# Expert stage: the next expert's down weights are split in an expert's last block, and GpSimd's wait for gathered rows moves

## The chip, the cores and the metric

The kernel runs on one core of a Trainium2 chip. Its time is the device time of one execution in microseconds. The core's engines are TensorE (PE; PEld is its weight load), VectorE (DVE), ScalarE (ACT), GpSimd (POOL) and SyncE (SP); each takes its own instructions in order and waits for others through semaphores.

## The reference, cut to what matters

The program is one step of a decoder layer: modulated RMSNorm, an input projection, two mixers, an output projection, and then a mixture of experts. The change lies in the experts alone. For 2056 tokens (2048 of a prompt, 8 samples), a router picks two of 32 experts for each. Each expert computes, on the rows sent to it,

```
def expert_mlp(xb, w1, w3, w2):
    return (jax.nn.silu(xb @ w1) * (xb @ w3)) @ w2
```

with `w1` (gate) and `w3` (up) of 1024 x 512 and `w2` (down) of 512 x 1024, all in fp32. An expert's weights are 6 MB. After the experts, each token's two rows are weighted, added to the residual and normalised.

## The kernel before, in words

Three sets of instructions make up the expert stage, in function `experts`. An expert's rows are cut into blocks of 128, and what is left over after the last full block goes, where it is few enough, into a small block of 32 rows. Experts are walked in order; a "run" is the stretch of experts between two small blocks, so that a small block always stands ahead of the first full block of its expert. How many blocks an expert has, and which have a small one, is known only on the chip: each engine reads it from an SBUF table (`entry`, line 2227, a register load) as it enters a run or an expert.

Precision: an fp32 matrix product is made of three products with shorter operands. ScalarE copies a weight half to `HI` (rounded, line 2344 in `upper(n, e)`), VectorE subtracts it from the raw weights to get `LO` (line 2422 in `lower(n, e)`), and TensorE adds up X_hi\*W_hi, X_lo\*W_hi and X_hi\*W_lo. Index n is 0 for gate, 1 for up, 2 for down; each has two halves of 128 x 2048. The raw weights are tile `WIDE` for gate and up and `W2E` for down; SyncE loads the next expert's half (line 2269) as soon as `LO` of the same half is made, and the small block, which reads raw weights, is done with it. There is one buffer of `HI` and of `LO` for each n.

A full block on TensorE (`block_`): 24 matmuls into `AE` (gate, line 2492), 24 into `BE` (up), six transposes of the next block's gathered rows `XG` into `XP` (line 2481), two transposes of the gated product (`GP`, line 2487), two more of `XP`, two more of `GP`, and 24 matmuls into `YP` (down, line 2497): eight with `HI`, eight with `GL` and `HI`, eight with `LO`. On ScalarE: `SE` = silu(AE) (line 2378), two casts `GH` of `GP` (2382), the cast `XH` of `XP` (2338), two copies `YE` of the output (2388), and its store (2390). On VectorE: `GE` = SE\*BE (2441), `GL` (2445), `XL` (2426). In an expert's last block the next expert's weights are split in between: `HI` of gate behind `SE`, `HI` of up behind `XH`; on VectorE `LO` of gate's first half ahead of `GE`, the rest behind `XL`. The down weights are split at the start of their own expert (`upper(2, e)`, `lower(2, e)`), ahead of `SE` on ScalarE and of everything on VectorE.

A small block (`small`): `AE` and `BE` from raw weights and `XS` (line 2506), `SS` = silu on ScalarE (2360), `GS` on VectorE (2431), a transpose `GP`, its copy `GTS` on ScalarE (2362), then `YP` from raw down weights (2506), `YS` (2368) and four stores (2372).

GpSimd fetches one block ahead (`fetch`): it loads row numbers to `IDX` (2288), waits for them, waits until TensorE has turned the former rows (`gather`), gathers `XG` (2284), and waits until they have landed. Between two runs it does the same for the small block with `IDXS` (2297) and `XGS` (2302). The time ends with a last stage (`combine_and_normalise`), which the change does not touch.

Of the kernel before, what the change touches and what calls it, by code (L numbers as in the profile page):

```python
# [37 lines left out]
KF = DEXP // P  # L38
# [2121 lines left out]
def experts(nc, t, dr, const, state):  # L2160
# [6 lines left out]
    T = SMALL_ROWS  # L2167
    with ExitStack() as ctx:
# [3 lines left out]
        def ps(name, shape):  # L2172
# [25 lines left out]
        sidx_in, sx_in, sx_turned, sx_ready, sa_done, ss_ready, sb_done, sg_ready, sg_turned, sgt_ready, sy_done, sy_taken, sy_out = (  # L2198
            sem(f"small_{x}") for x in ("idx_in", "x_in", "x_turned", "x_ready", "a_done", "s_ready", "b_done", "g_ready", "g_turned", "gt_ready", "y_done",
                                        "y_taken", "y_out"))  # L2200

        first_idx_in, first_x_in, first_turned = sem("first_idx_in"), sem("first_x_in"), sem("first_turned")
        table = state["blocks"]
        SEL, BASE = sb("SEL", [P, ALLT * 2, NEXP]), sb("BASE", [P, ALLT * 2])
        IDXS, IDX0, XG0 = sb("IDXS", [T, 1], I32), sb("IDXS0", [T, 1], I32), sb("XGS0", [T, D])
# [40 lines left out]
        with nc.Block() as block:  # L2246
# [28 lines left out]
            @block.gpsimd  # L2275
            def _(pool):
                def place(value, rows):
                    return nc.s_assert_within(pool.snap(value), 0, NEXP * CAP - rows,
                                              skip_runtime_bounds_check_because="an expert's blocks stay inside its CAP slots")

                def gather(b):
                    pool.wait_ge(x_turned, b + 1)
                    pool.sem_inc(fetching, 1)
                    pool.indirect_dma_start(XG[:], None, dr["h2"], bass.IndirectOffsetOnAxis(ap=IDX[:].bitcast(U32), axis=0)).then_inc(x_in, 16)  # L2284

                def fetch(e, first, skip, b):
                    slot = place(e * CAP + skip + (b - first) * P, P)
                    pool.dma_start(IDX[:], dr["slot"][ds(slot, P), :]).then_inc(idx_in, 16)
                    pool.wait_ge(idx_in, b * 16 + 16)
                    gather(b)  # L2290
                    pool.wait_ge(x_in, b * 16 + 16)

                def fetch_small(e, n):
                    slot = place(e * CAP, T)
                    pool.wait_ge(sx_in, pool.snap(n * 16 - 16))
                    pool.sem_inc(fetching, 1)
                    pool.dma_start(IDXS[:], dr["slot"][ds(slot, T), :]).then_inc(sidx_in, 16)
                    pool.wait_ge(sidx_in, n * 16)

                    pool.wait_ge(sx_turned, n)  # L2300
                    pool.sem_inc(fetching, 1)
                    pool.indirect_dma_start(XGS[:], None, dr["h2"], bass.IndirectOffsetOnAxis(ap=IDXS[:].bitcast(U32), axis=0)).then_inc(sx_in, 16)

                def fetch_expert(e):
                    first, end = bounds(pool, e)
                    skip = entry(pool, 3, e, 0, T)
                    with pool.Fori(first, end) as b:
                        fetch(e, first, skip, b)


                second = place(entry(pool, 0, 1, 1, LAST) * CAP, T)
                pool.dma_start(IDX0[:], dr["slot"][0:T, :]).then_inc(first_idx_in, 16)
                pool.dma_start(IDXS[:], dr["slot"][ds(second, T), :]).then_inc(sidx_in, 16)
                pool.wait_ge(first_idx_in, 16)
                pool.indirect_dma_start(XG0[:], None, dr["h2"], bass.IndirectOffsetOnAxis(ap=IDX0[:].bitcast(U32), axis=0)).then_inc(first_x_in, 16)
                pool.wait_ge(sidx_in, 16)
                pool.indirect_dma_start(XGS[:], None, dr["h2"], bass.IndirectOffsetOnAxis(ap=IDXS[:].bitcast(U32), axis=0)).then_inc(sx_in, 16)
                with pool.Fori(0, runs(pool)) as g:
                    head, behind = run(pool, g)
                    with pool.Fori(head, behind) as e:  # L2320
                        fetch_expert(e)
                    fetch_small(entry(pool, 5, g + 2, 0, LAST), pool.snap(g + 2))
                fetch_expert(LAST)
                blocks = entry(pool, 2, LAST, 1, MAXBLK)
                gather(blocks)

            @block.scalar
            def _(act):
# [45 lines left out]
                def block_(b, n, split):  # L2374
# [7 lines left out]
                        nc.scalar.copy(GH[:, half * 2:half * 2 + 2], GP[half][:]).then_inc(gh_ready, 1)  # L2382
                    take_x(b + 1)
                    split(1)
                    act.wait_ge(y_out, b * 16 + 16)
                    for half in range(2):
                        act.wait_ge(y_done, b * 2 + half + 3)
# [5 lines left out]
                upper(1, 0)  # L2393
                take_small(0)
                small(0, 0, lambda: take_x(0))
                number = runs(act)
                with act.Fori(0, number) as g:
                    head, behind = run(act, g)
                    with act.Fori(head, behind) as e:
                        upper(2, e)  # L2400
                        first, last = first_and_last(act, e)
                        with act.If(last > first):
                            with act.Fori(first, last) as b:
                                block_(b, g + 1, lambda n: None)
                        block_(last, g + 1, lambda n: upper(n, e + 1))
                    small(behind, g + 1)
                upper(2, LAST)
                first, end = bounds(act, LAST)
                with act.Fori(first, end) as b:
                    block_(b, number + 1, lambda n: None)  # L2410
# [6 lines left out]
            def _(dve):  # L2417
# [40 lines left out]
                with dve.Fori(0, number) as g:  # L2458
                    head, behind = run(dve, g)
                    with dve.Fori(head, behind) as e:  # L2460
                        lower(2, e)
                        first, last = first_and_last(dve, e)
                        with dve.If(last > first):
                            with dve.Fori(first, last) as b:
                                block_(b)
                        block_(last, dve.snap(e + 1))
                    small(g + 1)
                lower(2, LAST)
                first, end = bounds(dve, LAST)
                with dve.Fori(first, end) as b:  # L2470
                    block_(b)
                destinations(dve)
# [2 lines left out]
            def _(pe):  # L2475
# [49 lines left out]
                def small(e, n):  # L2525
# [13 lines left out]
                    if static:  # L2539
                        turn_small_g(n)  # L2540
                        turn_small(n + 1)
                        pe.wait_ge(x_in, 16)
                        pe.wait_ge(sx_ready, n + 2)
                        turn_x(range(KD)).then_inc(x_turned, 1)
                    else:
                        pe.wait_ge(xl_ready, first + 1)
                        turn_small(n + 1)
                        pe.wait_ge(gl_ready, first * 2 + 2)
                        turn_small_g(n)
# [12 lines left out]
                def block_(e, b, n):  # L2562
# [10 lines left out]
                    into_hidden(BP[:], XL, HI, 1)  # L2573
                    pe.wait_ge(lo_ready[1], e * 2 + 2)
                    into_hidden(BP[:], XH, LO, 1, last=True).then_inc(b_done, 1)
                    pe.wait_ge(x_in, b * 16 + 32)
                    turn_x(range(6))
                    pe.wait_ge(g_ready, b * 2 + 3)
                    turn_g(0)
# [11 lines left out]
                    into_rows(1, GH, HI, (2, 3))  # L2591
                    pe.wait_ge(gl_ready, b * 2 + 4)
                    for half in range(2):
                        into_rows(half, GL, HI, range(KF))
                    pe.wait_ge(lo_ready[2], e * 2 + 2)
                    for half in range(2):
                        into_rows(half, GH, LO, range(KF), last=True).then_inc(y_done, 1)
# [182 lines left out]
```

## Time and profile before

| | us |
|---|---|
| median of three runs | 2292.2 |
| lowest, highest | 2287.64, 2294.55 |
| the profiled execution's own time | 2288.98 |
| its span in the trace | 2287.5 |
| busy in the span: PE, DVE, ACT, POOL | 1968.3, 1610.8, 1072.1, 565.4 |

Durations are those of the one profiled execution, on a scale that starts with its span. The granted TensorE clock is 0.94 of 2.4 GHz over the whole span. The expert stage begins near 1330 us and its last full block ends near 2177 us. An engine's busy time says little here; what counts is what TensorE waits for, and which chain of waits goes round once in a block.

### The profile page before, as it was taken

The page shows a single profiled execution, that of the slowest core. Times are in us where ns is not written, and L with a number is a line of the kernel's source. Part 1 is how long each engine was busy: PE and PEld are TensorE (multiplying, and loading weights), DVE is VectorE, ACT ScalarE, POOL GpSimd, SP SyncE. Part 2 cuts the span into 40 slices and gives each one's busy share as a digit, 9 for nine tenths or more (in the row PEclk, how much of TensorE's full clock was granted, in tenths as well). Part 3 has the DMA queues.
Part 4 walks back from the last instruction along what each step waited for, and adds up shares of the span by engine and source line. Part 5 has one row for each costly group of instructions (what it writes and reads, how often), then busy time and mean ns, then how long its engine had stood idle before and what let it go on. Part 6 is the DMA issues. An engine that isn't in the chain of part 4 may idle for free. (4 is left out here: it accounts for less than half of the span.)

```text
span 2287.5 us, 40414 instructions
## 1 busy us (share of the span) xinstructions
PE 1968.3 (86%) x13004; PEld 1591.8 (70%) x13005; DVE 1610.8 (70%) x3113; ACT 1072.1 (47%) x2055; POOL 565.4 (25%) x558
## 2 busy tenths in 40 slices
PE   5999999999799998649999849999899999999900
PEld 3788888888577777427888738788777877878700
DVE  2567888889566667749999648766445676658778
ACT  2311111113577778314444237665445665647633
POOL 1024444441011111202655420101110101010066
PEclk7999999999899999869999969999999999999955
DMA  8755555554636448676787549977575978769787
GB/s 260 265 194 201 181 201 202 202 195 155 210 127 225 140 153 283 220 270 199 234 283 247 175 150 369 370 270 300 193 280 190 364 268 303 276 244 388 284 308 290
DMA packets 221577, 553.13 MB, mean 242 GB/s; under 512 B 28973, under 2 KB 43845, under 8 KB 220328
## 3 DMA queue, kind: packets, MB, share of 16 engines
q1 hardware_dynamic: 176272, 434.49, 54.1%
q0 software_dynamic: 24992, 75.13, 8.9%
q10 hardware_dynamic: 20224, 42.38, 5.2%
q8 instruction: 50, 0.82, 0.2%
q14 instruction: 39, 0.32, 0.0%
HBM read 456.86 MB, written 167.63 MB: 273 GB/s over the span
## 5 line engine op out<-in xcount | busy, mean ns | idle before, releaser
L2422 DVE TENSOR_TENSOR LO<-WIDE,HI 128x2048 fp32r<-128x2048 f32 x128 | 287.1, 2285 | 85.3 <-ACT HI L2344 85.3
L599 DVE SCALAR_TENSOR_TENSOR ARENA<-ARENA,TAPW 128x512 f32<-128x512 f32 (+3 forms) x493 | 293.4, 677 | 0.0
L2344 ACT CAST HI<-WIDE 128x2048 fp32r<-128x2048 f32 x128 | 237.8, 1909 | 18.7 <-PEq L199 16.2
L425 POOL TENSOR_TENSOR MS<-SSQ,K 128x1 f32<-128x1 f32 x17 | 167.8, 9869 | 295.2 <-ACT H L468 295.2
L2422 DVE TENSOR_TENSOR LO<-W2E,HI 128x2048 fp32r<-128x2048 f32 x64 | 143.8, 2289 | 93.5 <-ACT HI L2344 93.5
L718 PE MATMUL PJ<-WIN_H,HTH 128*128 128x512 f32 x680 | 173.4, 398 | 15.3 <-ACT HTH L474 11.7
L1044 ACT ACTIVATE PR<-SBX,NM 128x256 f32<-128x256 f32 (+1 forms) x384 | 171.9, 456 | 2.6 <-DVE NM L976 2.6
L722 PE MATMUL PJ<-WIN_H,HTL 128*128 128x512 f32 x680 | 169.7, 392 | 0.0
L726 PE MATMUL PJ<-WIN_L,HTH 128*128 128x512 f32 x680 | 168.1, 390 | 0.0
L500 ACT ACTIVATE ARENA<-PJ 128x512 f32<-128x512 f32 x51 | 30.4, 598 | 288.7 <-PE PJ L726 288.7
L718 PEld LDWEIGHTS PJ<-WIN_H,HTH 128*128 128x128 f32 x680 | 127.9, 190 | 46.5 <-ACT HTH L474 15.9
L722 PEld LDWEIGHTS PJ<-WIN_H,HTL 128*128 128x128 f32 x680 | 129.2, 190 | 27.2
L2344 ACT CAST HI<-W2E 128x2048 fp32r<-128x2048 f32 x64 | 119.2, 1910 | 61.1 <-issue 61.1
L726 PEld LDWEIGHTS PJ<-WIN_L,HTH 128*128 128x128 f32 x680 | 127.7, 188 | 26.5
L2284 POOL DMA_INDIRECT XG<-h_rows,IDX x41 | 47.2, 1150 | 330.2 <-PE XP L2481 263.3
L973 DVE CUSTOM_DVE_ANT_0 SBX<-S,WAD 128x256 f32<-128x256 f32 (+1 forms) x256 | 88.0, 400 | 33.9 <-issue 31.4
L1163 PE MATMUL OT<-PTS,VN 128*64 128x128 f32 x1200 | 90.2, 282 | 20.7 <-DVE PTS L986 20.7
L1140 PE MATMUL TB<-K,PR 128*128 128x128 f32 x600 | 85.4, 278 | 8.3 <-ACT PTS L1031 8.3
L1163 PEld LDWEIGHTS OT<-PTS,VN 128*64 128x64 f32 x1200 | 63.3, 136 | 41.5 <-issue 22.3
L942 POOL DMA_DIRECT2D branch_rows<-O x44 | 23.7, 540 | 266.6 <-ACT O L1025 266.6
L2492 PE MATMUL AE<-HI,XH 128*128 128x512 f32 x320 | 81.7, 398 | 8.6 <-issue 8.6
L2382 ACT CAST GH<-GP 128x256 fp32r<-128x256 f32 x80 | 29.8, 372 | 126.3 <-PE GP L2487 123.8
(341 smaller groups left out, 4359.5 us busy)
## 6 DMA issues: line engine op xcount, KB each, us to landing
WIDE<-in_w_expert_gate SPq DMA_DIRECT2D x64, 1024.0 KB, 7.5
WIDE<-in_w_expert_up SPq DMA_DIRECT2D x64, 1024.0 KB, 9.9
W2E<-in_w_expert_down SPq DMA_DIRECT2D x64, 1024.0 KB, 9.2
expert_rows<-YE ACTq DMA_DIRECT2D x40, 512.0 KB, 6.2
expert_rows<-NOROWS POOLq DMA_DIRECT2D x11, 1536.0 KB, 11.7
X<-in_x_prompt SPq DMA_DIRECT2D x31, 512.0 KB
WAD<-in_w_ada SPq DMA_DIRECT2D x13, 1024.0 KB, 8.6
QN<-q_rows SPq DMA_DIRECT2D x48, 256.0 KB, 3.0
```

The lines of the kernel that those rows point to most:

```text
L425: pool.tensor_tensor(MS[:], SSQ[:], const("eps"), ALU.add).then_inc(ms_ready, 1)
L599: ins = nc.vector.scalar_tensor_tensor(out=out, in0=src, scalar=tap, in1=out, op0=ALU.mult, op1=ALU.add)
L718: nc.tensor.matmul(PJ[:, n], HTH[:, k], WH[:, n, k], start=k == 0, stop=False)
L722: nc.tensor.matmul(PJ[:, n], HTL[:, k], WH[:, n, k], start=False, stop=False)
L726: mm = nc.tensor.matmul(PJ[:, n], HTH[:, k], WL[:, n, k], start=False, stop=k == KD - 1)
L973: nc.vector.tensor_tensor_reduce(SBX[hh][:, h, 0:wide], SP_[hh][:, at_bank(h), 0:wide], bias, 1.0, -3e38, ALU.add, ALU.max, ml[:, head:hea ...
L1044: ins = nc.scalar.activation(PR[hh][:, h, 0:w], SBX[hh][:, h, 0:w], ACT.Exp, bias=NM[:, head:head + 1], scale=1.0, accum_out=ML[g.q][:, HE ...
L1140: mm = nc.tensor.transpose(TB[u % 2][:, n], PR[head // HH][:, head % HH, k * P:(k + 1) * P], const("ident"))
L1163: mm = nc.tensor.matmul(OT[s * DH:(s + 1) * DH, pair], VN[(q - nk + 1 + k) % 4][:, head * DH:(head + 1) * DH], PTS[:, u, n], start=k == 0, ...
L2344: nc.scalar.copy(HI[n][:, cols], raw[n][:, cols]).then_inc(hi_ready[n], 1)
L2422: nc.vector.tensor_tensor(LO[n][:, cols], raw[n][:, cols], HI[n][:, cols], ALU.subtract).then_inc(lo_ready[n], 1)
L2492: mm = nc.tensor.matmul(out, x[:, k], w[n][:, k * DEXP:(k + 1) * DEXP], start=first and k == 0, stop=last and k == KD - 1)
```

## The change

On ScalarE, `upper(2, e + 1)` runs in the last block of expert e, behind `upper(1, e + 1)` and ahead of the two `YE` copies; it waits on a new semaphore, `down_used`, which TensorE raises after its last matmul of a block that reads `HI` of down. `upper(2, 0)` runs after the first small block, and the calls at an expert's start are gone. On VectorE, `lower(2, e)` stands where it was, at the start of its expert, but behind the table loads, and it waits for `y_done` of the block before. On GpSimd, the wait for the landed `XG` stands ahead of the next load of `IDX` instead of right behind the gather; the first load of row numbers counts on the same semaphore, which shifts its counts by 16.

```diff
                 def fetch(e, first, skip, b):
                     slot = place(e * CAP + skip + (b - first) * P, P)
+
+                    pool.wait_ge(x_in, b * 16 + 16)
+                    pool.sem_inc(fetching, 1)
                     pool.dma_start(IDX[:], dr["slot"][ds(slot, P), :]).then_inc(idx_in, 16)
                     pool.wait_ge(idx_in, b * 16 + 16)
                     gather(b)
-                    pool.wait_ge(x_in, b * 16 + 16)
...
                     take_x(b + 1)
                     split(1)
+                    split(2)
                     act.wait_ge(y_out, b * 16 + 16)
...
                 small(0, 0, lambda: take_x(0))
+                upper(2, 0)
                 number = runs(act)
+
+                def split_next(n, e, b):
+
+                    if n == 2:
+                        act.wait_ge(down_used, b + 1)
+                    upper(n, e + 1)
+
                 with act.Fori(0, number) as g:
                     head, behind = run(act, g)
                     with act.Fori(head, behind) as e:
-                        upper(2, e)
                         first, last = first_and_last(act, e)
...
-                        block_(last, g + 1, lambda n: upper(n, e + 1))
+                        block_(last, g + 1, lambda n: split_next(n, e, last))
                     small(behind, g + 1)
-                upper(2, LAST)
...
                     with dve.Fori(head, behind) as e:
+                        first, last = first_and_last(dve, e)
+
+                        dve.wait_ge(y_done, first * 2 + 2)
                         lower(2, e)
-                        first, last = first_and_last(dve, e)
...
                     for half in range(2):
-                        into_rows(half, GL, HI, range(KF))
+                        mm = into_rows(half, GL, HI, range(KF))
+                    mm.then_inc(down_used, 1)
                     pe.wait_ge(lo_ready[2], e * 2 + 2)
```

In ScalarE's program, the end of an expert's last block, before: `XH`, the next up weights' casts, the output copies and their store, then the loop's end.

```order
L2338 CAST XH<-XP 128x1024
L2344 CAST HI<-WIDE 128x2048 x2
L2385 ISA
L2388 COPY YE<-YP 128x512 x2
L2390 ISA
L2390 DMA expert_rows<-YE 128x1024
L2399 REGISTER_ALU
L2399 COMPARE_AND_BRANCH
```

The same place now:

```order
L2343 CAST XH<-XP 128x1024
L2349 CAST HI<-WIDE 128x2048 x2
L2349 CAST HI<-W2E 128x2048 x2
L2391 ISA
L2394 COPY YE<-YP 128x512 x2
L2396 ISA
L2396 DMA expert_rows<-YE 128x1024
L2413 REGISTER_ALU
L2413 COMPARE_AND_BRANCH
```

The two down casts have come in ahead of the copies and the store. In the same program, the start of an expert (the loop over the experts of a run), before; the table loads are `TENSOR_LOAD blocks`.

```order
L2399 ISA
L2344 CAST HI<-W2E 128x2048 x2
L2227 ISA
L2227 TENSOR_LOAD blocks
L2227 ISA x3
L2227 TENSOR_LOAD blocks
L2227 ISA x2
L2402 REGISTER_ALU
L2402 COMPARE_AND_BRANCH
```

And now:

```order
L2413 ISA
L2228 TENSOR_LOAD blocks
L2228 ISA x3
L2228 TENSOR_LOAD blocks
L2228 ISA x2
L2415 REGISTER_ALU
L2415 COMPARE_AND_BRANCH
```

The two table loads used to stand behind the casts; now nothing is ahead of them but the store of the former block.

## Rows read from the trace of the kernel before

**Rows 1.** Experts' stretch: length; busy PE, PEld, DVE, ACT, POOL; clock; DMA share; GB/s.

```profile
1355.00:2170.00 815.00, 783.82 (x4886) 638.05 (x4887) 530.92 (x393) 488.58 (x461) 86.13 (x97) 0.99 0.79 292
```

**Rows 2.** PE's waits there: us in total, times, longest.

```profile
PE XP L2481 <- DMA XG<-h_rows,IDX: 15.3, 3, 6.8
PE GP L2487 <- DVE GE L2441: 5.4, 6, 1.1
PE YP L2506 <- ACT GTS L2362: 4.0, 9, 0.4
```

**Rows 3.** Timeline of a block ahead of a single-block expert: start, us, engine, operation.

```profile
1387.64 0.60 ACT L2378 ACTIVATE SE<-AE 128x512 f32<-128x512 f32 x1
1388.13 3.70 ACT L2344 CAST HI<-WIDE 128x2048 fp32r<-128x2048 f32 x2
1390.27 2.29 DVE L2422 TENSOR_TENSOR LO<-WIDE,HI 128x2048 fp32r<-128x2048 f32 x1
1393.15 0.75 DVE L2441 TENSOR_TENSOR GE<-SE,BE 128x256 f32<-128x256 f32 x2 [0.60 <-PE BE L2492]
...
1395.72 3.72 ACT L2344 CAST HI<-WIDE 128x2048 fp32r<-128x2048 f32 x2
...
1400.38 0.59 ACT L2388 COPY YE<-YP 128x512 f32<-128x512 f32 x1 [0.26 <-PE YP L2497]
1401.24 0.38 ACTq L2390 DMA_DIRECT2D expert_rows<-YE  x1
1402.08 3.73 ACT L2344 CAST HI<-W2E 128x2048 fp32r<-128x2048 f32 x2 [1.11 <-issue]
...
1405.82 0.60 ACT L2378 ACTIVATE SE<-AE 128x512 f32<-128x512 f32 x1
```

**Rows 4.** TensorE's two late transposes of gathered rows.

```profile
1651.32 1.54 PE L2481 MATMUL XP<-K,XG 128*128 128x128 f32 x6 [5.50 <-DMA XG<-h_rows,IDX]
...
1926.76 0.87 PE L2481 MATMUL XP<-K,XG 128*128 128x128 f32 x6 [2.96 <-DMA XG<-h_rows,IDX]
```

**Rows 5.** GpSimd's gathers: two behind the small block at 1627, one of 1920.

```profile
1632.19 0.86 POOL L2302 DMA_INDIRECT XGS<-h_rows,IDXS  x1 [17.94 <-PE XP L2518]
...
1642.73 2.88 POOL L2284 DMA_INDIRECT XG<-h_rows,IDX  x1 [5.83 <-DMA IDX<-slot_tokens]
...
1920.28 1.04 POOL L2284 DMA_INDIRECT XG<-h_rows,IDX  x1 [5.47 <-DMA IDX<-slot_tokens]
```

**Rows 6.** Timeline around the small block at 1627.

```profile
1622.53 3.72 ACT L2344 CAST HI<-WIDE 128x2048 fp32r<-128x2048 f32 x2
...
1628.01 0.34 ACTq L2390 DMA_DIRECT2D expert_rows<-YE  x1
...
1629.25 0.28 ACT L2360 ACTIVATE SS<-AE 128x128 f32<-128x128 f32 x1 [1.50 <-PE AE L2506]
1630.89 0.29 DVE L2431 TENSOR_TENSOR GS<-SS,BE 128x128 f32<-128x128 f32 x1 [0.38 <-PE BE L2506]
1632.07 1.93 PE L2506 MATMUL YP<-W2E,GTS 128*32 128x256 f32 x32 [0.45 <-ACT GTS L2362]
...
1638.33 3.72 ACT L2344 CAST HI<-W2E 128x2048 fp32r<-128x2048 f32 x2 [3.84 <-issue]
1640.27 4.49 DVE L2422 TENSOR_TENSOR LO<-W2E,HI 128x2048 fp32r<-128x2048 f32 x2 [9.09 <-ACT HI L2344]
```

**Rows 7.** ScalarE's table loads in 1636.6 to 1638.3, before the casts: min/median/max ns.

```profile
L2227 ACTq TENSOR_LOAD <-blocks x2: 280/280/281, 1637.0 to 1637.6; - x2
```

**Rows 8.** The gathers of `XG` in 1355 to 2170, ns, and their landing.

```profile
L2284 POOL DMA_INDIRECT XG<-h_rows,IDX x40: 944/972/3047, 1362.8 to 2146.1; - x40
...
DMA to landing us min/median/max: 4.0/6.7/8.8
```

**Rows 9.** SyncE's loads of down weights: one pair, and the landing of all.

```profile
1388.29 2.46 SPq L2269 DMA_DIRECT2D W2E<-in_w_expert_down  x2
...
DMA to landing us min/median/max: 4.8/9.2/10.9
```

More of the change, by code:

```diff
@@ L2200, in experts @@
                                         "y_taken", "y_out"))
-        first_idx_in, first_x_in, first_turned = sem("first_idx_in"), sem("first_x_in"), sem("first_turned")
+        down_used = sem("down_hi_used")
+        first_x_in, first_turned = sem("first_x_in"), sem("first_turned")
         table = state["blocks"]
@@ L2311, in _ @@
                 second = place(entry(pool, 0, 1, 1, LAST) * CAP, T)
-                pool.dma_start(IDX0[:], dr["slot"][0:T, :]).then_inc(first_idx_in, 16)
+                pool.dma_start(IDX0[:], dr["slot"][0:T, :]).then_inc(x_in, 16)
                 pool.dma_start(IDXS[:], dr["slot"][ds(second, T), :]).then_inc(sidx_in, 16)
-                pool.wait_ge(first_idx_in, 16)
+                pool.wait_ge(x_in, 16)
                 pool.indirect_dma_start(XG0[:], None, dr["h2"], bass.IndirectOffsetOnAxis(ap=IDX0[:].bitcast(U32), axis=0)).then_inc(first_x_in, 16)
@@ L2324, in _ @@
                 blocks = entry(pool, 2, LAST, 1, MAXBLK)
+                pool.wait_ge(x_in, blocks * 16 + 16)
                 gather(blocks)
@@ L2467, in _ @@
                     small(g + 1)
+                first, end = bounds(dve, LAST)
+                dve.wait_ge(y_done, first * 2 + 2)
                 lower(2, LAST)
-                first, end = bounds(dve, LAST)
                 with dve.Fori(first, end) as b:
@@ L2541, in small @@
                         turn_small(n + 1)
-                        pe.wait_ge(x_in, 16)
+                        pe.wait_ge(x_in, 32)
                         pe.wait_ge(sx_ready, n + 2)
@@ L2575, in block_ @@
                     into_hidden(BP[:], XH, LO, 1, last=True).then_inc(b_done, 1)
-                    pe.wait_ge(x_in, b * 16 + 32)
+                    pe.wait_ge(x_in, b * 16 + 48)
                     turn_x(range(6))
```

## The prediction

> **What bounds the kernel now.** I read the busy time by stretch first, then TensorE's waits, then the timeline of single blocks. In the 815 us of the experts TensorE is busy for 783.8 us at a granted clock of 0.99, with 0.79 of the DMA engines' time taken [rows 1]. So TensorE sets the pace, and what the change can give is what TensorE now waits: 15.3 us for gathered rows in three waits, of which the first, 6.8 us, is the start of the stage; 5.4 us for `GE` in six; 4.0 us for `GTS` in nine [rows 2]. No wait for `HI`, `LO` or raw weights of the down projection is among them. The nine waits for `GTS` are the nine small blocks behind the first, so small blocks are places where TensorE has nothing to do while ScalarE works.
>
> The timeline gives a second picture, the loop that ScalarE and VectorE go round once in a block. From one `SE` to the next it is 1405.82 - 1387.64 = 18.18 us [rows 3], which is TensorE's own period of a block. `GE` is made ready by TensorE: VectorE sat idle 0.60 us for `BE` ahead of it [rows 3]. That 0.60 us is all the slack that this loop has in a single-block expert, since there VectorE makes `LO` of the next gate's first half between `SE` and `GE`.
>
> **The row numbers on GpSimd.** The two late transposes inside the stage (5.50 and 2.96 us) [rows 4] hang on this chain: TensorE turns the small block's rows, the gather of `XGS` starts (1632.19, waited 17.94 us for TensorE), table loads, the load of `IDX`, its landing, the gather of `XG` at 1642.73 [rows 5]. The wait that the change moves stands before the 17.94 us of waiting and is hidden by it. The row numbers of a small block will be loaded some 5 to 7 us earlier and nothing behind it starts earlier. Elsewhere the gathers already wait for TensorE. Gain: 0; an added semaphore step in each fetch lies in the same waits.
>
> **The down split: small blocks.** Ahead of a small block, ScalarE's casts of `HI` for up start at 1622.53 and last 3.72 us [rows 6]. Now two more casts of the same length follow (2 x 3.72 = 7.44, to 1629.97), then two copies `YE` of 0.59 us. Neighbours overlap by about 0.1 us (`SE` starts at 1387.64, lasts 0.60, and its successor starts at 1388.13 [rows 3]), so the copies end near 1630.9. The store starts 0.27 us behind the last copy (1400.38 + 0.59 to 1401.24 [rows 3]), near 1631.15, and `SS` 1.24 us behind the store (1628.01 to 1629.25 [rows 6]), near 1632.4 in place of 1629.25. It lasts 0.28 us, and `GS` follows near 1632.7 in place of 1630.89: 1.8 us late. From `GS` to TensorE's `YP` nothing has room (1.18 us, and TensorE sat idle for `GTS` [rows 6]), so TensorE loses 1.8 us. Bounds: 1.6 if the 1.24 us holds some waiting for `AE`, 2.2 if nothing overlaps. Nine small blocks: **+16.2** (14.4 to 19.8). The next down weights must have landed for this; see the rivals.
>
> **The down split: what goes.** Behind a small block, `HI` and `LO` of down are now ready or in work before the block begins; before, the casts stood at 1638.33, ahead of `SE` [rows 6]. That is what made `GE` late in six blocks, by up to 1.1 us [rows 2]; all six waits are in the first block behind a small one. The casts kept `SE` back until 1642.05 (1638.33 + 3.72); without them it can start about 2 us earlier, even with its table loads bare. Gain: **-5.4** (at least -4).
>
> **Gathered rows after that.** In both places of [rows 4] a small block stands between the fetch and the late transpose, so 1.8 us of each wait is filled by the small block's new delay, which costs nothing there: 5.50 becomes 3.7, 2.96 becomes 1.2. Besides, the gather at 1642.73 took 2.88 us, three times the median of 0.972, and lay beside `LO` of down, which stood there from 1640.27 for 4.49 us [rows 6] and will now follow `GS` and be done by 1638; landing in the median 6.7 us in place of the 8.5 that its late start and the transpose at 1651.32 give takes off 1.8 more [rows 4, 5, 8]. At 1920 the gather was near its normal length and only its transfer has less company: I take 0.6 off. Sum: 8.46 less (1.9 + 0.6) = **-6.1**; bounds -3.6 (only the filling) and -8.5 (all of it goes).
>
> The Trainium skill speaks against the middle part of this. "SBUF — State Buffer", under "Practical consequences", says that a `tensor_tensor` with two SBUF inputs takes only the read side of the interface shared with GpSimd, and infers that making descriptors needs the write side, so that this operation did not stall a DMA. By that rule the 2.88 us is not `LO`'s doing and the sum would be 1.8 us higher. This trace speaks for a hold-up: the longest gathers [rows 8] all lie beside a `LO`.
>
> **The down split: single-block experts.** This is the part that is easy to miss. The two table loads of an expert ran under the down casts; now they stand bare between the store and `SE`. From `HI` of up at 1395.72: 7.44 us of casts, 1.18 of copies, less 0.3 of overlap, to 1404.1; the store at 1404.4; then 0.84 us as now from the store to what follows it (1401.24 to 1402.08 [rows 3]); then two loads of 0.28 us each, with their register steps 1.33 us (1637.0 to 1638.33 [rows 6, 7]); and 0.25 us for the branch and the row address. `SE` at 1406.8 in place of 1405.82: 1.0 us late. From `SE` to the earliest `GE` is 0.49 + 2.14 + 2.29, less 0.1 of overlap, 4.8 us [rows 3], so `GE` at 1411.6 to 1411.7 where TensorE has it due at 1393.15 + 18.18 = 1411.33. The loop becomes 18.5 us long and TensorE waits 0.3 to 0.4 us in each round. An expert pays it if it has one full block and no small block: 15 such experts by the order of `SE` and down casts in the trace, the first with casts at 1383.91, the last at 2134.88. At 0.35: **+5.2**. Bounds: 0, if a few tenths of my steps overlap, and 0.8 each, 12, if the loads or the branch take twice as long. An expert of several blocks does not pay, since its first block has no `LO` ahead of `GE`.
>
> The output copies come 3.5 us later, but TensorE needs `YP` only in the next block's last third, so that is free. VectorE's `LO` of down ends 8 us into the block as before.
>
> **Sum.** 16.2 - 5.4 - 6.1 + 5.2 = +9.9 us on the profiled execution's 2288.98, which is 2298.9. That execution lies 3.2 us below the median of the runs, so the forecast for a median is 2292.2 + 9.9 = **2302**.
>
> **Rivals.**
> - The loop of single-block experts keeps pace (0 in place of 5.2). For it: 0.3 us is less than the sum of what I read off in six steps. Against: all six steps are in the rows. +4.7: 2297. Chance 0.20.
> - The down weights land late. A pair is issued at 1388.29, the second half near 1390.4 [rows 9]; the casts now want them near 1399.4 and 1401.2. With the median landing of 9.2 us there are 1.6 us left; with the longest, 10.9, the cast waits 0.1 us, and a queue with less room would make it more. In single-block experts each tenth goes into the loop. At 0.7 us more in 15: +20, 2312. Chance 0.14.
> - The other side: the late `SS` is not what TensorE waits for in a small block, and the five or more us of `GE` and the row waits go in full. TensorE's waits would fall by 8.5 + 5.4 = 13.9, and at 0.5 us for each small block the sum is -9.4: 2283. It decides from the point where a small block costs less than 1.5 us. Against it: in [rows 6] only 1.2 us lie between `GS` and `YP`, and all of it is work. Chance 0.06.
> - The gather at 1642.73 stays long for a reason other than `LO`: 1.8 us of the row waits stay, +11.7, 2304. Chance 0.10. The Trainium skill's rule named above ("SBUF — State Buffer") would have it so.
>
> **How the numbers follow.** My case has 0.50, with a range of its own of 2297 to 2308. The low sum of all bounds is 14.4 - 5.4 - 8.5 + 0 = +0.5, the high one 19.8 - 4 - 3.6 + 12 = +24.2: 2293 to 2316. The range reaches from 2293 to 2315; the case of the other side is left out. A measurement of this kernel can tell about 0.3%, 6.9 us, from no change: below 2285.3 is faster, above 2299.1 slower. Slower: most of my case and of the long gather's, and the late weights, 0.67. The same: the loop that keeps pace and the low end of my case, 0.27. Faster: 0.06.
>
> **What would show it.** In the new profile `GTS` waits of TensorE should be about 2.2 us each, nine times, in place of 0.45. The waits for `GE` behind small blocks should be gone, and some 15 of 0.3 us should stand in their place, with `SE` 6.8 us into a block in place of 5.9. The wait of GpSimd for TensorE ahead of `XGS` should be longer and the transposes near 1651 and 1927 late by 2 us and 1 us. I am wrong on the mechanism if the nine `GTS` waits stay near 0.45 us, or if TensorE now waits for `HI` or `LO` of down.

## The result and the profile after

The changed kernel takes 2297.15 us, the median of 13 runs (2292.87 to 2302.28); the kernel before takes 2290.7 us in 13 runs of the same sittings (2282.33 to 2294.55). The ratio is 1.0038, with a 95% interval of 1.0028 to 1.0048: the change costs 8.7 us (6.4 to 11.0), where +9.9 was forecast. The profiled execution of the new kernel spans 2295.4 us, that of before 2287.5.

TensorE's waits in the experts' stretch (1355 to 2190) show the exchange. Columns: what waited and for what, us in total, times, longest.

```profile
PE GP L2538 <- DVE GS L2443: 14.7, 9, 1.7
PE XP L2496 <- DMA XG<-h_rows,IDX: 9.8, 3, 5.9
PE AE L2507 <- issue: 5.0, 6, 1.5
PE YP L2521 <- ACT GTS L2367: 4.0, 9, 0.4
PE GP L2502 <- DVE GE L2453: 0.9, 3, 0.4
```

Against [rows 2], the wait for gathered rows is down from 15.3 to 9.8 us (0.9 of this at the start of the stage, 6.8 against 5.9), that for `GE` from 5.4 to 0.9. A new line stands on top: in each of the nine small blocks TensorE now waits up to 1.7 us for `GS`. The wait for `GTS` is what it was. There is no wait for `HI` or `LO` of down. The wait "for issue" of 1.5 us is that ahead of the stage's first full block; the others, 0.7 to 0.8 us each, stand ahead of a full block behind a small one.

A small block, start, us, engine and operation, to be laid beside [rows 6]:

```profile
1621.84 3.72 ACT L2349 CAST HI<-WIDE 128x2048 fp32r<-128x2048 f32 x2
1625.45 3.72 ACT L2349 CAST HI<-W2E 128x2048 fp32r<-128x2048 f32 x2
...
1626.40 1.95 PE L2521 MATMUL AE<-WIDE,XS 128*32 128x128 f32 x64
...
1630.39 0.34 ACTq L2396 DMA_DIRECT2D expert_rows<-YE  x1
...
1631.63 0.28 ACT L2365 ACTIVATE SS<-AE 128x128 f32<-128x128 f32 x1 [1.50 <-issue]
1631.94 0.29 DVE L2443 TENSOR_TENSOR GS<-SS,BE 128x128 f32<-128x128 f32 x1 [2.12 <-ACT SS L2365]
1632.38 0.30 PE L2538 MATMUL GP<-K,GS 128*128 128x128 f32 x1 [1.66 <-DVE GS L2443]
1633.12 3.45 PE L2521 MATMUL YP<-W2E,GTS 128*32 128x256 f32 x32 [0.45 <-ACT GTS L2367]
...
1635.89 4.49 DVE L2434 TENSOR_TENSOR LO<-W2E,HI 128x2048 fp32r<-128x2048 f32 x2 [3.66 <-issue]
1636.50 2.22 PE L2507 MATMUL AE<-HI,XH 128*128 128x512 f32 x8
```

`SS` follows `HI` of up by 9.79 us; the forecast's steps give 1632.4 - 1622.53 = 9.87. TensorE stands 1.66 us for `GS`. Then something that no step of the forecast had: the 32 matmuls of `YP` take 3.45 us, where those of before took 1.93 [rows 6].

The windows of the same trace say why. Columns: stretch, length, busy PE, PEld, DVE, ACT, POOL, granted clock, DMA share, GB/s. The first lies behind the small block above, the second behind another one of the same kernel.

```profile
1634.00:1637.00 3.00, 3.00 (x27) 1.52 (x19) 1.11 (x1) 0.33 (x1) 0.58 (x1) 0.53 0.98 363
1750.00:1753.00 3.00, 3.00 (x13) 2.50 (x14) 2.91 (x2) 0.00 (x0) 0.00 (x0) 1.00 1.04 413
```

A clock of 0.53 is nearly all at the lower level, 1.2 GHz. Such a stretch of 3.4 us stands behind four of the nine small blocks (at 1633.4, 1848.4, 1913.3 and 1944.0), where the 32 matmuls take 3.00 to 3.45 us; the other five run them in 1.93 us, as all nine did before. Where the stretch begins late, it reaches into the next full block, whose first eight matmuls then take up to 2.65 us in place of 2.09:

```profile
1850.68 2.62 PE L2507 MATMUL AE<-HI,XH 128*128 128x512 f32 x8
```

A block ahead of a single-block expert, to be laid beside [rows 3]:

```profile
1398.44 1.98 PE L2507 MATMUL AE<-HI,XH 128*128 128x512 f32 x8
...
1402.56 0.38 ACTq L2396 DMA_DIRECT2D expert_rows<-YE  x1
...
1405.02 0.60 ACT L2383 ACTIVATE SE<-AE 128x512 f32<-128x512 f32 x1 [2.74 <-PE AE L2507]
...
1407.45 2.29 DVE L2434 TENSOR_TENSOR LO<-WIDE,HI 128x2048 fp32r<-128x2048 f32 x1 [1.10 <-ACT HI L2349]
1409.66 0.74 DVE L2453 TENSOR_TENSOR GE<-SE,BE 128x256 f32<-128x256 f32 x2
...
1416.64 1.98 PE L2507 MATMUL AE<-HI,XH 128*128 128x512 f32 x8
```

`SE` follows the store by 2.46 us with no cast between: those are the bare table loads. `GE` follows `SE` by 4.64 us and VectorE no longer sits idle for `BE` ahead of it, so the slack of 0.60 us [rows 3] is used up. Yet TensorE's round is 1416.64 - 1398.44 = 18.20 us, hardly longer than the 18.18 of before. It becomes clearly longer only where the loads themselves are slow, as in the block that starts at 2084.02, a round of 18.62 us:

```profile
2091.02 0.60 ACT L2383 ACTIVATE SE<-AE 128x512 f32<-128x512 f32 x1 [3.17 <-issue]
...
2096.12 0.44 PE L2502 MATMUL GP<-K,GE 128*128 128x128 f32 x2 [0.40 <-DVE GE L2453]
```

The two table loads there, and all of the stretch (min/median/max ns):

```profile
L2228 ACTq TENSOR_LOAD <-blocks x2: 452/579/706, 2089.0 to 2089.8; - x2
```
```profile
L2228 ACTq TENSOR_LOAD <-blocks x87: 273/285/761, 1385.3 to 2169.6; - x87
```

Of the 15 rounds of single-block experts, two are 0.44 and 0.47 us longer than before (mean of their two loads 0.53 and 0.58 us) and four are 0.16 to 0.21 us longer (0.42 to 0.48 us). The other nine, with loads of 0.38 us or less in the mean, are longer by at most 0.07 us.

Of [rows 4], the two late transposes are still late, by 2.29 and 1.59 us in place of 5.50 and 2.96, and the gathers of [rows 8] are all short now:

```profile
1650.07 1.23 PE L2496 MATMUL XP<-K,XG 128*128 128x128 f32 x6 [2.29 <-DMA XG<-h_rows,IDX]
...
1929.25 0.87 PE L2496 MATMUL XP<-K,XG 128*128 128x128 f32 x6 [1.59 <-DMA XG<-h_rows,IDX]
```
```profile
L2285 POOL DMA_INDIRECT XG<-h_rows,IDX x40: 946/972/982, 1361.5 to 2152.6; - x40
```

To size each term I took the starts of TensorE's blocks in each trace (the first matmul of every `AE`, and of `YP` in small blocks) and summed the distances by kind, from the first full block's start to the last one's. The same blocks are in the same column for every kernel; all in us.

| kernel | small: `AE` to `YP` (9) | small: `YP` to next `AE` (9) | first block | six blocks that waited for `GE` | two blocks that waited for rows | 15 single-block experts | rest | total |
|---|---|---|---|---|---|---|---|---|
| before | 45.17 | 23.52 | 19.77 | 115.57 | 46.99 | 272.77 | 272.92 | 796.71 |
| after | 60.19 | 25.85 | 18.28 | 110.91 | 42.37 | 274.69 | 272.80 | 805.09 |
| difference | +15.0 | +2.3 | -1.5 | -4.7 | -4.6 | +1.9 | -0.1 | +8.4 |

The 8.4 us covers what the two spans differ by (7.9) and agrees with the ratio (8.7), so the change acts in this stretch.

The first block's 1.5 us is no wait. Its first eight matmuls ran at the lower clock in the trace of before and not in the new one:

```profile
1362.23 3.54 PE L2492 MATMUL AE<-HI,XH 128*128 128x512 f32 x8 [2.44 <-issue]
```
```profile
1361.98 2.10 PE L2507 MATMUL AE<-HI,XH 128*128 128x512 f32 x8 [1.45 <-issue]
```

The granted clock in 1362 to 1365 is 0.50 before and 1.00 after.

### The profile page after: what moved, and what is told of

It is laid out like the page before. It is cut to its first block and busy times, and to the rows that moved or that the text cites. A ratio compares the mean times of both kernels' runs of the same rounds, so it can differ in the third digit from the quotient of the medians.

```text
span 2295.4 us, 40488 instructions
## 1 busy us (share of the span) xinstructions
PE 1976.1 (86%) x13004; PEld 1595.9 (70%) x13005; DVE 1610.3 (70%) x3113; ACT 1063.1 (46%) x2055; POOL 556.4 (24%) x558
## 5 line engine op out<-in xcount | busy, mean ns | idle before, releaser
L2349 ACT CAST HI<-WIDE 128x2048 fp32r<-128x2048 f32 x128 | 237.3, 1909 | 16.2 <-PEq L199 16.2
L2285 POOL DMA_INDIRECT XG<-h_rows,IDX x41 | 39.8, 971 | 451.5 <-PE XP L2496 424.3
L2383 ACT ACTIVATE SE<-AE 128x512 f32<-128x512 f32 x40 | 24.0, 599 | 152.9 <-PE AE L2507 123.9
L2512 PE MATMUL YP<-HI,GH 128*128 128x512 f32 x320 | 83.7, 404 | 4.6
```

The costliest lines, as they stand in the source:

```text
L2349: nc.scalar.copy(HI[n][:, cols], raw[n][:, cols]).then_inc(hi_ready[n], 1)
L2512: mm = nc.tensor.matmul(YP[:, half * 512:half * 512 + 512], g[:, k], w[2][:, k * D + half * 512:k * D + half * 512 + 512], start=first and ...
```

## The experiments

Theory A, from the prediction: the casts ahead of small blocks cost, their absence behind small blocks gains, the loop of single-block experts is at its limit, and GpSimd's edit is worth nothing. Rivals: the cost is GpSimd's and not the split's; the loop has slack left and the loss is all in small blocks; the long gathers are not `LO`'s doing; the half clock behind small blocks is what the runs' difference is made of. The first four kernels stand beside the same runs of before (median 2290.64 us), and so do the last four (2287.32 us).

| kernel | median us | ratio to before, 95% interval | profiled span |
|---|---|---|---|
| pool_only | 2287.11 | 0.9984 [0.9968, 0.9999] | 2288.6 |
| split_only | 2300.32 | 1.0041 [1.0022, 1.0061] | 2305.4 |
| casts_in_small | 2284.79 | 0.9974 [0.9959, 0.9989] | 2288.3 |
| loads_doubled | 2321.42 | 1.0133 [1.0107, 1.0160] | 2320.6 |
| inner_early | 2282.74 | 0.9978 [0.9961, 0.9994] | 2284.6 |
| warm | 2295.44 | 1.0027 [1.0009, 1.0045] | 2298.3 |
| numbers_early | 2278.97 | 0.9964 [0.9948, 0.9980] | 2275.2 |
| all_moves | 2269.96 | 0.9926 [0.9899, 0.9953] | 2263.6 |

And their blocks, in the columns of the table above. It is one trace each, so a column moves by chance too; and the column of single-block experts holds one late transpose of the first run in split_only (about 2.0 us) and in casts_in_small (9.1 us), which is no loss of the loop.

| kernel | small `AE` to `YP` | `YP` to `AE` | first | six `GE` | two rows | 15 single | rest | total |
|---|---|---|---|---|---|---|---|---|
| pool_only | 45.15 | 23.65 | 19.85 | 115.13 | 49.29 | 272.89 | 272.92 | 798.88 |
| split_only | 60.68 | 27.52 | 19.78 | 111.96 | 40.48 | 279.16 | 272.84 | 812.42 |
| casts_in_small | 45.17 | 23.50 | 18.27 | 111.32 | 47.37 | 281.86 | 272.84 | 800.33 |
| loads_doubled | 59.90 | 26.55 | 18.29 | 110.17 | 43.46 | 299.83 | 272.84 | 831.04 |
| inner_early | 45.16 | 23.64 | 19.91 | 110.11 | 48.96 | 275.93 | 272.76 | 796.47 |
| warm | 60.83 | 23.68 | 19.64 | 109.78 | 45.56 | 276.44 | 272.81 | 808.74 |
| numbers_early | 45.18 | 23.50 | 19.88 | 115.41 | 38.65 | 272.66 | 272.84 | 788.12 |
| all_moves | 45.18 | 23.55 | 18.31 | 111.41 | 37.82 | 272.63 | 272.81 | 781.71 |

### The two parts apart: pool_only and split_only

pool_only is the kernel before with GpSimd's edit alone:

```diff
 def fetch(e, first, skip, b):
     slot = place(e * CAP + skip + (b - first) * P, P)
+    pool.wait_ge(x_in, b * 16 + 16)
+    pool.sem_inc(fetching, 1)
     pool.dma_start(IDX[:], ...).then_inc(idx_in, 16)
     pool.wait_ge(idx_in, b * 16 + 16)
     gather(b)
-    pool.wait_ge(x_in, b * 16 + 16)
```

> The kernel before with GpSimd's edit alone. My theory: the moved wait stands ahead of a wait for TensorE (17.94 us at 1632), so TensorE's time does not change: 0, and the transposes near 1651 and 1927 are late by 5.5 and 3.0 us as before. Rival (the edit removes row waits): both waits go, -8.5 us.

Measured: 0.9984 [0.9968, 0.9999]. Its trace shows the waits of before in sum, three for rows of 15.4 us together and six for `GE`:

```profile
PE XP L2484 <- DMA XG<-h_rows,IDX: 15.4, 3, 6.6
...
PE GP L2490 <- DVE GE L2444: 4.8, 6, 0.8
```

So the cost of the change isn't in this edit. The two late transposes wait 8.8 us together, for 8.5 before, as forecast; but one by one they are not those of before:

```profile
1648.05 1.54 PE L2484 MATMUL XP<-K,XG 128*128 128x128 f32 x6 [3.11 <-DMA XG<-h_rows,IDX]
...
1925.32 1.54 PE L2484 MATMUL XP<-K,XG 128*128 128x128 f32 x6 [5.66 <-DMA XG<-h_rows,IDX]
```

The long gather has changed places with them: 1.02 us at 1641.60 and 3.08 us at 1916.36, for 2.88 and 1.04 in [rows 5]. Whether the edit gains up to 0.3% in another way is at the limit of what the runs tell.

split_only is the new kernel with the same lines put back as they were before; the down split stays.

> The changed kernel with GpSimd's part undone. My theory: as slow as the changed kernel, +8 to +9 us against before, with nine waits of 1.6 us for GS in small blocks. Rival (GpSimd's part gave something back): 3 us or more slower than the changed kernel.

Measured: 1.0041 [1.0022, 1.0061], +9.4 us, which is all of the change's cost. The rival, a kernel 3 us slower than the changed one, lies inside the interval and isn't excluded. In its trace `AE` to `YP` of the small blocks is 60.68 us, as in the new kernel, so that +15 belongs to the split. Its waits:

```profile
PE GP L2535 <- DVE GS L2440: 15.0, 9, 1.7
PE XP L2493 <- DMA XG<-h_rows,IDX: 12.7, 5, 6.9
```

Two things are different from the new kernel. There are five waits for rows in place of three; one of the new ones (1.91 us, at 1470.66) stands in the first run of experts. And the half clock stands behind eight of the nine small blocks (`YP` to next `AE` 27.52 us).

### Where the down casts of a small block's expert should stand: casts_in_small

The kernel before, with one group of casts moved: those for an expert that comes behind a small block are made inside it, behind `SS`, where ScalarE has room. All others stay at the start of their expert.

```diff
@@ small, on ScalarE
         meanwhile()
+    upper(2, e)
     act.wait_ge(sy_out, n * 64 + 64)
@@ loop over experts
-    upper(2, e)
+    with act.If(e > head):
+        upper(2, e)
@@ ahead of the last expert
-upper(2, LAST)
```

> The kernel before, but the down casts of an expert with a small block run in that small block, behind ScalarE's copies of GTS, XS and XH; all other experts cast at their start as before. My theory (the changed kernel's gain is the six GE waits and the held-up gather, its cost the late SS): no GS waits, no GE waits, the gather near 1643 back at 1.0 us and its wait down from 5.5 to about 3.7: -5.4 - 1.9 - about 1 at the first block = -7 to -8 us. Rival (the GE waits come from something else than the order on ScalarE): 0.

Measured: 0.9974 [0.9959, 0.9989], -6.0 us for the -7 to -8 expected. This takes the split's gain without its price: `AE` to `YP` stays at 45.17 us, the six blocks fall to 111.32, and TensorE waits 0.8 us for `GE`:

```profile
PE XP L2482 <- DMA XG<-h_rows,IDX: 20.9, 4, 6.7
...
PE GP L2488 <- DVE GE L2442: 0.8, 4, 0.2
```

The trace itself is no shorter than before's in this stretch (800.33 against 796.71), because of a wait for rows in the first run that the trace of before doesn't have:

```profile
1468.36 1.54 PE L2482 MATMUL XP<-K,XG 128*128 128x128 f32 x6 [6.74 <-DMA XG<-h_rows,IDX]
```

GpSimd ahead of it:

```profile
1443.64 0.56 POOL L2297 DMA_DIRECT2D IDXS<-slot_tokens  x1 [9.06 <-issue]
1449.14 1.28 POOL L2302 DMA_INDIRECT XGS<-h_rows,IDXS  x1 [4.93 <-DMA IDXS<-slot_tokens]
1453.26 0.58 POOL L2288 DMA_DIRECT2D IDX<-slot_tokens  x1 [2.84 <-issue]
1459.72 2.31 POOL L2284 DMA_INDIRECT XG<-h_rows,IDX  x1 [5.89 <-DMA IDX<-slot_tokens]
```

Four steps stand in a row, and a gather of 2.31 us beside `LO` ends them. In the new kernel, with GpSimd's edit, the first of these is 12 us earlier and the gather waits for TensorE:

```profile
1431.34 0.56 POOL L2300 DMA_DIRECT2D IDXS<-slot_tokens  x1 [0.54 <-issue]
...
1448.07 0.97 POOL L2285 DMA_INDIRECT XG<-h_rows,IDX  x1 [5.59 <-PE XP L2496]
```

That is where GpSimd's edit has a use: it gives the first run's fetches 12 us of room that they need only sometimes. Both kernels whose trace has this wait lack the edit; that the edit's small gain in pool_only is made of it is likely, but wasn't shown.

### Does the loop of single-block experts have slack: loads_doubled

The new kernel, with the two table loads ahead of `SE` made twice:

```diff
     with act.Fori(head, behind) as e:
+        first_and_last(act, e)
         first, last = first_and_last(act, e)
```

> The changed kernel with the two table loads at an expert's start done twice on ScalarE, 1.3 us more between store and SE. If the loop SE, HI, LO, GE, HI, HI, SE has used up its slack, as its GE now stands 0.07 us behind TensorE's pace, each of 15 single-block experts without a small block pays 1.2 to 1.3 us: +18 us on the changed kernel, and more waits of TensorE for GE. Rival (TensorE sets the pace there with room to spare): 0 to +3 us.

Measured: 1.0133 [1.0107, 1.0160], 24 us above the new kernel in medians, for the +18 expected. The 15 single-block experts take 299.83 us, 25.1 more than in the new kernel, 1.68 each, and nothing else moved by more than 1.1. TensorE's waits for `GE`:

```profile
PE GP L2503 <- DVE GE L2454: 21.4, 15, 2.3
```

Fifteen waits for `GE`, as many as there are such experts: more time on ScalarE between the store and `SE` goes into TensorE's time, so the loop has no slack left in the new kernel. The forecast had the mechanism and the count right and the size too low. The waits are 1.43 us each; the rest of the loss is mostly the clock, which was at 0.50 to 0.53 in 3 us behind three of the longest of them (2.26, 1.60 and 2.14 us), where the round took 1.4 to 1.7 us more than its wait. The new kernel's own loss there is small because it stands just at the limit.

### The new kernel without its casts ahead of small blocks: inner_early

Here the new kernel keeps the early split between two experts of a run, and makes that for a small block's expert inside the small block. The call `upper(2, 0)` behind the first small block is gone too (not shown below).

```diff
@@ small, on ScalarE
+    upper(2, e)
@@ split_next
-    if n == 2:
-        act.wait_ge(down_used, b + 1)
-    upper(n, e + 1)
+    if n < 2:
+        upper(n, e + 1)
+    else:
+        with act.If(behind > act.snap(e + 1)):
+            act.wait_ge(down_used, b + 1)
+            upper(2, act.snap(e + 1))
```

> The changed kernel, but an expert with a small block has its down casts in that small block, behind ScalarE's copies; only experts without one keep the split in the block before. My theory: the small blocks' 15 us and the half-clock stretches behind them are gone, and what is left against the kernel with casts in small blocks alone is the loop of single-block experts, 0.05 to 0.4 us in each of 15, +1 to +5 us on it, about -3 to 0 us against before. Rival (the whole loss came from the small blocks): the same time as casts in small blocks alone, -6 us.

Measured: 0.9978 [0.9961, 0.9994], -5.0 us for the -3 to 0 expected, against 1.0038 for the new kernel: the casts ahead of small blocks, with what follows from them, cost 0.6%. `AE` to `YP` is back at 45.16 and `YP` to `AE` at 23.64 us, so the half clock has gone with the wait. The 15 experts take 275.93, 3.2 more than before: in this trace, the loop's price alone. Its waits:

```profile
PE XP L2499 <- DMA XG<-h_rows,IDX: 15.3, 3, 6.9
PE GP L2505 <- DVE GE L2456: 2.2, 3, 1.0
```

The waits for rows are back at 15.3 us, 8.4 of it in the two late transposes (6.9 is the first), although the down `LO` is made early here too and the gather is short. The first of the two, GpSimd's step and TensorE's:

```profile
1639.63 0.97 POOL L2285 DMA_INDIRECT XG<-h_rows,IDX  x1 [5.61 <-DMA IDX<-slot_tokens]
```
```profile
1647.07 1.54 PE L2499 MATMUL XP<-K,XG 128*128 128x128 f32 x6 [4.27 <-DMA XG<-h_rows,IDX]
```

The other waits 4.18 us, for 2.96 before, although its gather was short both times. So one wait of one trace tells little, and the two late transposes have to be read over several kernels. Where the gather was long (2.88 and 3.08 us: before, pool_only) they waited 5.50 and 5.66 us. Where it was short and the small blocks as before (before, pool_only, casts_in_small, inner_early) the six waits lie between 2.96 and 4.27 us, 3.7 in the mean. Where it was short and the small block late (the new kernel, split_only, loads_doubled, warm) the eight lie between 1.49 and 3.77 us, 2.2 in the mean. So the long gather costs some 1.8 us, and the small block's delay fills some 1.5 us of each wait, which is no true gain. In time inner_early and casts_in_small can't be told apart.

### Is it the clock: warm

The new kernel, with five matmuls of 512 columns that nobody reads, in the small block's wait for `GS`. They add work and take none out.

```diff
     turn_small(n + 1)
+    pe.wait_ge(hi_ready[0], e * 2 + 2)
+    pe.wait_ge(y_taken, first * 2 + 2)
+    pe.wait_ge(sy_taken, n + 1)
+    for k in range(5):
+        nc.tensor.matmul(YP[:, 0:512], XH[:, k], HI[0][:, ...], start=k == 0, stop=k == 4)
```

> The changed kernel with five matmuls of 512 columns, whose result is thrown away, in the wait for GS of each small block. The wait of 1.65 us is still there as time. If the half clock behind small blocks (four stretches of 3.4 us in the changed kernel's trace) comes from TensorE's idling there, no such stretch is left and the time falls by 3 to 5 us on the changed kernel. Rival (the clock falls for another reason, or the filler delays more than it saves): stretches remain, 0 to +3 us on the changed kernel.

Measured: 1.0027 [1.0009, 1.0045]. In the trace the half clock is gone from behind all nine small blocks, and `YP` to next `AE` takes 23.68 us in place of 25.85:

```profile
1631.23 1.43 PE L2567 MATMUL YP<-HI,XH 128*128 128x512 f32 x5
...
1633.74 1.93 PE L2521 MATMUL YP<-W2E,GTS 128*32 128x256 f32 x32 [0.45 <-ACT GTS L2367]
```
```profile
1634.00:1637.00 3.00, 2.33 (x35) 1.47 (x28) 0.28 (x1) 0.37 (x1) 0.00 (x0) 1.00 0.94 315
```

So it is the idle time in the small block that lets the clock fall. Its price in the new kernel's trace is 2.3 us between `YP` and `AE` and some 1.1 us in two of the six blocks behind (18.83 and 18.87 us in place of 18.3; none over 18.33 in warm). `AE` to `YP` is unchanged at 60.83: most of the cost is the late `GS` and not the clock. By the ratios warm is 2.5 us faster than the new kernel, for the 3 to 5 expected, but the two intervals overlap, so the runs don't show it; and its trace as a whole is 3.7 us longer, by waits for rows (6.2 us for 3.9), the first block and the loop.

### What the late gathers really wait for: numbers_early

The kernel before; the row numbers of the next run's first block are loaded ahead of GpSimd's wait for the turned small rows, not behind it. This is the wait of 17.94 us in [rows 5] that the change's own edit doesn't pass.

```diff
 def fetch_small(e, n, following):
     ...
     pool.dma_start(IDXS[:], ...).then_inc(sidx_in, 16)
+    first_numbers(following)
     pool.wait_ge(sidx_in, n * 16)
     pool.wait_ge(sx_turned, n)
@@ fetch
+    with pool.If(b > begun):
+        numbers(e, first, skip, b)
     pool.wait_ge(idx_in, b * 16 + 16)
     gather(b)
```

> The kernel before, but GpSimd loads the row numbers of the next run's first block ahead of its wait for the small block's rows to be turned. My theory: the late transposes near 1651 and 1927 hang on the chain turned, gather, table loads, row numbers, gather; with the row numbers there beforehand both waits (5.5 and 3.0 us) go, and the odd one in the first run: -8 to -10 us. Rival (the gathers' transfers are what is late): less than -3 us.

Measured: 0.9964 [0.9948, 0.9980], -8.2 us, at the near end of the -8 to -10 expected. The two blocks with late rows fall from 46.99 to 38.65 us. That this 8.3 is nearly the 8.46 of [rows 4] is chance: the waits are gone, and with them some 1.6 us of lower clock behind the longer one (the clock was 0.56 in 1652 to 1656 before), but two waits for `GE` of 0.81 and 0.90 us, which they had covered, came out. Beyond the start of the stage there is no wait for rows left:

```profile
PE GP L2498 <- DVE GE L2452: 6.9, 8, 1.0
```

The chain of [rows 5] is thus shown to be the cause of those waits.

### Together: all_moves

The kernel before with the three edits that gained or did no harm: casts_in_small, the change's own edit on GpSimd, and numbers_early.

> Casts in small blocks, GpSimd's deferred wait, and the early row numbers together, on the kernel before. The waits for GE and for rows are different stretches, so the gains add up: -6 (casts) - 7 (rows, less what the casts already gave there) = -12 to -15 us. Rival (what one gives, the next wait takes): no better than the better of the two alone.

Measured: 0.9926 [0.9899, 0.9953], 2269.96 us: 17 us faster than before, for the -12 to -15 expected, and the fastest of all. The single ratios add up to 0.9974 + 0.9964 + 0.9984 - 2 = 0.9922. TensorE's waits for `GE`:

```profile
PE GP L2501 <- DVE GE L2455: 2.0, 7, 0.5
```

The row numbers stand ready before the gather, and a gather beside `LO` (1.92 us) no longer matters, since it starts 5.25 us behind the start of `XGS` in place of 10.54 [rows 5]:

```profile
1621.29 0.90 POOL L2312 DMA_INDIRECT XGS<-h_rows,IDXS  x1 [20.50 <-issue]
1626.54 1.92 POOL L2284 DMA_INDIRECT XG<-h_rows,IDX  x1 [4.35 <-issue]
```

## Why the prediction was right, and where it was not

The forecast of +9.9 us and the measured +8.7 (6.4 to 11.0) agree, and the median of 2297.15 us lies in the stated range, 4.9 us under the 2302 named (1.5 of it because the median of before fell to 2290.7 with more runs). The largest term and its mechanism are the ones foretold. That the sum comes out so near is in part luck: of the new kernel's trace, the single-block experts are 3.3 us less than forecast, and the clock, which was in no term, is about as much more. The chance of 0.67 was for more than 2299.1 us, which the median doesn't reach; that the kernel is slower is clear only because 13 runs of each give a narrow interval. Point by point:

- **Small blocks, +16.2.** Measured +15.0, 1.67 each for 1.8. Shown by split_only (there) and by inner_early (gone with the casts). The sign foretold was the wrong one: the new wait shows at the transpose of `GS`, with 14.7 us in nine, while the nine waits for `GTS` stay at 0.45, which the prediction had named as proof that its mechanism was wrong. `GTS` is made from what TensorE transposes, so it can't take on a delay that comes from `GS`; the mechanism held, and the sign didn't follow from it.
- **`GE` behind small blocks, -5.4.** Measured -4.7, which holds about +1.1 of the lower clock; without that stretch the same six blocks gain 5.8 (warm) and 5.5 (inner_early). casts_in_small gets 4.3 alone, without the early split.
- **Gathered rows, -6.1.** Measured -4.6, within its bounds (its own terms, 8.46 less 1.9 and 0.6, give -6.0 and not -6.1). Both parts are there: the gather did get shorter (2.88 us became 0.97), worth some 1.8 us by the waits of all traces, as foretold, and the small block's delay laid over the waits took some 1.5 us from each, for 1.8. The waits of one trace scatter by as much as these parts, so the nearness of the sum says less than they do.
- **Single-block experts, +5.2.** This is the term that was mis-sized: measured +1.9 in the new kernel, nearer to the rival's 0 than to the forecast, 3.2 and 3.7 in inner_early and warm. `SE` was as late as foretold (0.94 us for 1.0; it stands 6.58 us into the block for 5.64, where the prediction has 6.8 for 5.9). But `GE` follows it by 4.64 us, not 4.8, which leaves a normal round 0.02 us long; only rounds with slow table loads pay more, two of them 0.4 to 0.5 and four about 0.2, and three waits for `GE` show in place of 15. The step that failed was the difference of two nearly equal times, each with some 0.1 us of reading error. loads_doubled shows the mechanism itself, and that the loop, where it keeps pace, does so only by a hair.
- **The clock.** No term of the sum had it. It costs 2.3 us between `YP` and the next `AE` in the new kernel's trace (4.0 in split_only) and about 1.1 in the blocks behind, and warm shows its cause.
- **The first block, -1.5.** In the trace of before its first matmuls ran at the lower clock. It is near 19.8 us in six of the ten traces, with 3.18 to 3.63 us for these eight matmuls, and near 18.3 in the other four, with 2.09 to 2.11. warm, which has all of the change, is among the six, so it is chance and not the change's.
- **GpSimd's edit, 0.** pool_only shows no gain at the late transposes, 8.8 us for 8.5. Its 0.9984 [0.9968, 0.9999] leaves up to 0.3%, which the forecast didn't see.
- **The long gather.** The trace of before had all its long gathers beside a `LO`; with `LO` of down ahead of it, the new kernel's gather fell to 0.97 us. In all ten traces, 35 gathers of `XG` took over 1.0 us, and every one of them lay at least in part beside a `LO`. The rival that it has another cause finds no support, and neither, in this kernel, does the inference of the Trainium skill ("SBUF — State Buffer", "Practical consequences") that a `tensor_tensor` with two SBUF inputs doesn't stall the making of descriptors. What is open is when a `LO` does it: three gathers nearly wholly beside one took 0.97 to 0.98 us (before at 1455.94, the new kernel at 1933.26, loads_doubled at 1664.40), and no run moved a `LO` alone.

The other rivals: no cast waited for late down weights in the new trace; the case of the other side had its condition (a small block under 1.5 us) refuted by 1.67.

## What to carry to other kernels

Moving work ahead of a wait is paid by whatever stood behind it: ask at every place where the moved work lands (here the last block ahead of a small one, and that ahead of another full one) which deadline follows, and move it only where there is room; the casts of a small block's expert, moved into the small block behind `XS`, turned +0.4% into -0.2% (inner_early). Before a wait is moved, look for the longest wait on that engine: what has to pass it is the load of row numbers behind 17.94 us of waiting, and not the one that the change moved. And where a forecast rests on a slack of a few tenths, double the suspected cost once: loads_doubled told in one run that the loop is at its limit.

## What the runs showed of the hardware

- TensorE's clock fell to its lower level (granted clock 0.50 to 0.53) for about 3.4 us behind some small blocks in which TensorE had sat idle 1.66 and 0.45 us, in an otherwise full stretch: behind four of nine in the new kernel, eight of nine in split_only, four of nine in loads_doubled (there once with 0.89 and 0.45 us), and none where the idle time was 0.45 us alone (before, inner_early) or was mostly filled by matmuls (warm). It fell also behind three of the 15 waits for `GE` in loads_doubled (2.26, 1.60 and 2.14 us). The same kernel does it at one place and not at another, with the same waits ahead; what decides stays open.
- GpSimd's indirect gather takes 0.97 us, and up to 3.05 us (before), 3.08 (pool_only), 3.06 (split_only) and 3.09 (casts_in_small) when VectorE runs `LO`, a subtraction with both inputs in SBUF. `LO` itself isn't longer for it, 2.28 to 2.34 us in all 188 of before. In no trace was a gather of `XG` that lay apart from `LO` longer than 0.99 us; three beside one weren't either.
- A load of a table value to a register on ScalarE took 0.273 to 0.761 us in the new kernel (median 0.285). In the kernel before they ran under the casts, and `SE` followed the casts without a gap [rows 3]; bare behind the store, two of them and the steps around them put `SE` 0.94 us later.
